# Delta rule: the first convolution tap moves to ScalarE, keys times beta becomes one VectorE operation, and the planner's durations follow

## The chip, the core and the metric

The kernel runs on one core of a Trainium2 chip. The core has TensorE (matrix products; the profile calls it PE, and PEld its loading of weights), VectorE (DVE), ScalarE (ACT), GpSimd (POOL) and SyncE (SP, which here only issues DMAs). Each engine takes its instructions strictly in the order of its own program and waits on semaphores for the others. The metric is the device time of one execution in microseconds; the median of several executions counts.

## What is computed

Two layers of one transformer block (convolutions, differential attention, SwiGLU) and then a second block with a gated delta rule, band attention, attention to a memory and SwiGLU, over 512 positions of width 1024, all in fp32. The change lies in the delta rule of the second block. Its part of the reference, cut to what matters:

```python
qkv = jax.nn.silu(_causal_dwconv(jnp.concatenate([qa, ka, va], axis=-1), conv_w[l]))   # 4 taps
q = _l2norm(...) * (A_DK ** -0.5);  k = _l2norm(...)          # 8 heads, chunks of 64
beta = sigmoid(beta);  g = -exp(a_log) * softplus(alpha + dt_bias);  G = cumsum(g)
L = where(strict, beta[..., :, None] * (k @ k.T) * decay, 0)
rhs = concatenate([beta[..., None] * v, (beta * exp(G))[..., None] * k], -1)
u_t, w = split(triangular_solve(I + L, rhs))
p_intra = (q @ k.T) * decay;  q_dec = q * exp(G);  k_dec = k * exp(g_last - G)
# scan over the 8 chunks: U = u_t - w @ S; o = q_dec @ S + p_intra @ U; S = S * e + k_dec.T @ U
```

The convolution has four taps per channel: position t gets tap 3 times itself plus taps 2, 1 and 0 times the three positions before it.

## The kernel before

Every large product is a *unit*: a weight matrix of 128 x 2048 numbers in `WR`, loaded by SP, split by ScalarE into a high part `WH` (step `split`, line 2191, one operation of 128 x 2048) and by GpSimd into a low part `WL` (step `low`, line 3036, eight operations of 128 x 256). TensorE multiplies activations (high and low part, `HH` and `HL`) with them at line 1894. The split of a unit waits until TensorE has finished the unit two before it, because the two share a buffer.

In the delta rule (`deltanet`) the projections of q, k and v come out of such units, and everything else is woven between them. For head h and j in q, k, v:

- `dq1` (VectorE, line 2783): the projection's bank times the row norm, into `pad`, of which there are two;
- `dq2` (VectorE), four steps with k = 3, 2, 1, 0: the first (line 2791) writes pad times tap 3 into `c`; it waits for `dq1` and, through `c_after`, for the readers of the old `c`. The others (line 2794) add one shifted tap each;
- `dq3` (ScalarE, line 2324): SiLU in place.

`prepare(h)` then makes what the solve and the scan need. In it `p9` multiplies the keys, which TensorE has turned into a bank, by the per-position factor in `RC[:, i, 2, h]`, one VectorE operation for each of four blocks of 128 columns, into `bk` (line 2840); ScalarE then makes `KD` from the same bank in four operations (line 2354). `invert(g)` solves for two heads at a time with 64 small products of 32 x 32 per step (lines 2034, 2044, 2053 and 2064), between which VectorE masks, subtracts and transposes (2868 to 2891). `scan(g)` runs the eight chunks (TensorE lines 2086, 2095, 2104 and 2112; VectorE 2906 and 2918; ScalarE 2377 and 2382).

The order of all steps is made at build time. `weave` keeps one clock per engine (`Clock`) and a lane for each generator, and always lets the lane go on whose last step ends first; the dense products are the first lane, whose time is that of TensorE. What a step costs on each engine is written in the table `ROUGH` (pairs of a fixed and a growing part, V for VectorE, A for ScalarE, T for TensorE). `Clock.run` starts a step when its engine is free and what it waits for is done. All engines' programs are emitted from the one list of steps, so a changed entry in `ROUGH` can change the order of instructions on each engine, but not their number.

Of the kernel before, what the change touches and what calls it, by code (L numbers as in the profile page):

```python
# [10 lines left out]
ALU = mybir.AluOpType  # L11
ACT = mybir.ActivationFunctionType
AX = mybir.AxisListType.X

P = 128
S = 512
# [78 lines left out]
def memory(nc, ctx):  # L95
# [153 lines left out]
    "gates1": ("V:ab", "A:beta"), "soft1": ("V:dtb", "A:edt", "A:alog"), "soft2": ("V:udt", "A:ldt"), "soft3": (),  # L249
    "gates3": ("V:dcum", "V:rg", "V:rlast", "A:reg", "A:rdec"),  # L250
    "gates4": ("A:rct",), "gates5": ("A:rhi", "V:rlo"),
    "nt": ("V:nt",), "dq1": ("V:dq1",), "dq2": ("V:dq2",), "dq3": ("A:dq3",),
    "p1": ("A:p1q",), "p2": ("A:pks",), "peq": ("V:peq",), "prow": (), "p4": ("V:p4a", "V:p4", "A:pdec"), "p4n": ("V:pkn",), "p4d": ("V:pdn",),
    "p5": (), "p6": ("V:psq",), "p6v": ("A:pbv",),
    "p8": (), "p9": ("V:pbk", "A:pkd"), "p11": (), "p12": ("V:pum",), "p13": (),
# [64 lines left out]
def by_dma(unit):  # L320
# [110 lines left out]
class Order:  # L431
# [6 lines left out]
    def step(self, kind, *key, **given):  # L438
        ends = self.pass_time(kind, key, given)
        for signal in KINDS[kind]:  # L440
            engine, name = signal.split(":")
            assert (name, key) not in self.value, (name, key)
            sem = SEMAPHORE.get(name, name)
            self.count[sem] = self.count.get(sem, 0) + 1
            self.value[name, key] = self.count[sem]
            self.last[engine] = (sem, self.count[sem])
            self.clock.when[self.last[engine]] = ends.get(engine, ends["end"])
        self.steps.append((kind, key, given))
# [42 lines left out]
    def at(self, name, *key):  # L491
        return SEMAPHORE.get(name, name), self.value[name, key]
# [49 lines left out]
def order(m):  # L542

    o = Order()
    at, step, now = o.at, o.step, o.now
# [6 lines left out]
    vec = lambda name, j=0: m.VECS[:, VEC[name] + j:VEC[name] + j + 1]  # L552
# [535 lines left out]
    def deltanet(fo, res_toks):  # L1088
# [57 lines left out]
        cfree = {n + str(i): f for n in "qkv" for i in range(2)}  # L1146
# [36 lines left out]
        def convolutions():  # L1183

            for h in range(8):
                for j in range(3):
                    while (h, j) not in pad_of:
                        yield
                    yield from until((read[j], h - 2))
                    pd = pad_of[h, j]  # L1190
                    for k in (3, 2, 1, 0):
                        step("dq2", h, j, k, pad=pd.i, tok=at("dq1", h, j), c_after=cfree["qkv"[j] + str(h % 2)])
                        if k == 0:
                            pd.free(at("dq2", h, j, 0))
                        yield
                    step("dq3", h, j)
                    curved[j].add(h)
                    yield
# [654 lines left out]
def blk(t, b):  # L1853
    return t[:, b * P:(b + 1) * P]


def v4(ap):
    return ap.rearrange("p (b q) -> p b q", q=P)
# [317 lines left out]
def scalar_program(nc, m, o, sems):  # L2176
    a, at = nc.scalar, o.at
    ae = Waits(a, sems)
    PB = m.PB
    vec = lambda name, j=0: m.VECS[:, VEC[name] + j:VEC[name] + j + 1]  # L2180
# [3 lines left out]
    for kind, key, w in o.steps:  # L2184
# [13 lines left out]
        elif kind == "gain":  # L2198
            site, c = key
# [11 lines left out]
        elif kind == "sq":  # L2211
            site, i, c = key
# [39 lines left out]
        elif kind == "glub":  # L2252
            l, j = key
            ae.wait_ge(*at("glu2", l, j))
            a.activation(m.ct[:], m.ct[:], ACT.Sigmoid, bias=vec(f"glu_b{l}", 2 + j)).then_inc(sems["glu3"], 1)
        elif kind == "lnact":
            l, j = key
            ae.wait_ge(*at("lnmul", l))
            a.activation(m.cc[j][:], m.cc[j][:], ACT.Silu, bias=vec(f"ln_b{l}", j), scale=vec(f"ln_g{l}", j)).then_inc(sems["lnact"], 1)
        elif kind == "qkin":  # L2260
            l, name, c = key
# [13 lines left out]
        elif kind == "sexp":  # L2275
            l, h, qb = key
            i, n = w["i"], P * (qb + 1)
            sums = (m.sm[:, 72 + 4 * h + qb:73 + 4 * h + qb], m.sm[:, 16 * i + 5:16 * i + 6])
            for j in range(2):
                ae.wait_ge(*at(f"smax{j}", *key))  # L2280
                ins = a.activation(m.pa[i][j][:, 0:n], m.pa[i][j][:, 0:n], ACT.Exp, bias=m.sm[:, 16 * i + j:16 * i + j + 1], scale=-1.0,
                                   accum_out=sums[j])
            ins.then_inc(sems["sexp"], 1)
        elif kind == "strans":
            l, h, qb = key
# [3 lines left out]
        elif kind == "spv":  # L2289
            l, h, qb = key  # L2290
# [26 lines left out]
        elif kind == "gates5":  # L2317
            ae.wait_ge(*at("rg"))
            a.activation(m.RHL[0:32, :], m.R[0:32, :], ACT.Copy)
            a.activation(m.RHL[64:96, :], m.R[64:96, :], ACT.Copy).then_inc(sems["rhi"], 1)  # L2320
        elif kind == "dq3":
            h, j = key
            ae.wait_ge(*at("dq2", h, j, 0))
            a.activation(m.cqkv[h % 2][j][:], m.cqkv[h % 2][j][:], ACT.Silu).then_inc(sems["dq3"], 1)
        elif kind == "p1":
            h, = key
# [3 lines left out]
        elif kind == "p2":  # L2330
            h, = key
            ae.wait_ge(*w["tile"].done)
            ae.all(w["after"])
            for i in range(4):
                ins = a.activation(blk(m.SQ[w["q"]], i), blk(PB[w["tile"].b], i), ACT.Square, accum_out=norms(h, 0)[:, i:i + 1])
# [4 lines left out]
        elif kind == "p6v":  # L2340
            h, = key
# [3 lines left out]
            for i in range(4):  # L2345
                ins = a.activation(blk(m.bv[h % 2], i), blk(PB[w["tile"].b], i), ACT.Copy, scale=norms(h, 2)[:, i:i + 1])
            ins.then_inc(sems["pbv"], 1)
        elif kind == "p9":
            h, = key
# [3 lines left out]
            for i in range(4):  # L2353
                ins = a.activation(m.KD[g][:, h % 2, i * P:(i + 1) * P], blk(PB[w["tile"].b], i), ACT.Copy, scale=norms(h, 3)[:, i:i + 1])
            ins.then_inc(sems["pkd"], 1)
        elif kind == "jd":
# [3 lines left out]
            for i in range(4):  # L2360
                rows = slice(32 * i, 32 * i + 32)
                ins = a.activation(diagonal(i, i), blocks(m.ZC[rows, :]), ACT.Copy)
# [4 lines left out]
        elif kind in ("i8u", "i8w"):  # L2367
            h, = key
# [15 lines left out]
        elif kind == "zact":  # L2384
            h, = key
            ae.wait_ge(*at("za1", h))
            a.activation(m.zs[h % 2][:], m.zs[h % 2][:], ACT.Silu).then_inc(sems["za"], 1)
        elif kind == "gact":
            c, = key
# [3 lines left out]
        elif kind == "bvin":  # L2393
            p, j = key
# [3 lines left out]
        elif kind == "bexp":  # L2398
            c, i, qb = key
# [4 lines left out]
        elif kind == "btrans":  # L2404
            c, i, qb = key
# [3 lines left out]
        elif kind == "bpv":  # L2409
            c, qb = key  # L2410
# [3 lines left out]
        elif kind == "gbact":  # L2414
            c, = key
            ae.wait_ge(*at("gb1", c))
            a.activation(m.SGB[:, c, :], m.SGB[:, c, :], ACT.Tanh, scale=0.5).then_inc(sems["gb"], 1)
        elif kind == "yop":
            _, c = key
# [7 lines left out]
        elif kind == "mssq":  # L2427
            c, = key
            ae.all(w["after"])
            a.activation(m.SQ[w["q"]][:, 0:256], m.MT[:, c, :], ACT.Square).then_inc(sems["mssq"], 1)  # L2430
        elif kind == "mop":
            _, c = key
# [3 lines left out]
        elif kind == "mvin":  # L2436
            u, j = key
# [4 lines left out]
        elif kind == "xexp":  # L2442
            h, qb = key
            i, j = h % 2, qb % 2
# [4 lines left out]
        elif kind == "xcopy":  # L2449
            h, = key  # L2450
# [4 lines left out]
        elif kind == "xpv":  # L2455
            h, k = key
# [5 lines left out]
def vector_program(nc, m, o, sems):  # L2462
    v, at = nc.vector, o.at
    ve = Waits(v, sems)
    dv = Chain(ve, "vchain")
    PB = m.PB
    ident = m.CON[:, C_ID:C_ID + P]
    vec = lambda name, j=0: m.VECS[:, VEC[name] + j:VEC[name] + j + 1]
# [33 lines left out]
    for kind, key, w in o.steps:  # L2502
# [3 lines left out]
        elif kind == "gain":  # L2506
            site, c = key
# [7 lines left out]
        elif kind == "sq":  # L2515
            site, i, c = key
# [7 lines left out]
        elif kind == "res":  # L2524
            name, c = key
# [52 lines left out]
        elif kind == "lam":  # L2578
# [3 lines left out]
            for j in range(2):  # L2582
# [3 lines left out]
                ins = v.tensor_reduce(sm[:, b + j:b + j + 1], sm[:, 64 + 64 * j:128 + 64 * j], AX, ALU.add)  # L2586
# [12 lines left out]
        elif kind == "glua":  # L2599
            l, j = key  # L2600
# [5 lines left out]
        elif kind == "glub":  # L2606
            l, j = key
            ve.all(w["after"])
            times_rstd(m.ct[:], w["tile"], "glu2")
        elif kind == "gluc":  # L2610
            l, j = key
# [7 lines left out]
        elif kind == "tap":  # L2619
            l, k, j = key  # L2620
# [163 lines left out]
        elif kind == "dq2":  # L2784
            h, j, k = key
            c, pad = m.cqkv[h % 2][j], m.pad[w["pad"]]
            tap = vec("conv2", 24 * k + 8 * j + h)
            if k == 3:
                ve.wait_ge(*at("dq1", h, j))
                ve.all(w["c_after"])  # L2790
                v.tensor_scalar(c[:], pad[:, 3:3 + S], tap, None, ALU.mult).then_inc(sems["dq2"], 1)
            else:
                ve.wait_ge(*at("dq2", h, j, k + 1))
                v.scalar_tensor_tensor(c[:], pad[:, k:k + S], tap, c[:], ALU.mult, ALU.add).then_inc(sems["dq2"], 1)
        elif kind == "p4":
            h, = key
            ve.wait_ge(*w["tile"].done)
# [37 lines left out]
        elif kind == "p9":  # L2835
            h, = key
            ve.wait_ge(*w["tile"].done)
            ve.all(w["after"])
            for i in range(4):
                ins = v.tensor_scalar(blk(m.bk[h % 2], i), blk(PB[w["tile"].b], i), m.RC[:, i, 2, h:h + 1], None, ALU.mult)  # L2840
            ins.then_inc(sems["pbk"], 1)
        elif kind == "p12":
            h, = key
            ve.wait_ge(*w["tile"].done)
# [385 lines left out]
```

## Time and profile before

| | us |
|---|---|
| median of 3 runs | 2467.93 (2467.66 to 2469.52) |
| the profiled execution | 2474.92 |
| its span in the trace | 2473.3 |

Busy shares of the span: PE 98%, PEld 81%, DVE 41%, ACT 38%, POOL 48%. Time is in us and duration of one operation in ns. The delta rule fills about 1160 to 1633 us of the span. A window row gives the busy time of each engine in that stretch with its count of instructions, then the granted TensorE clock (1.00 is 2.4 GHz; the other level is 1.2 GHz, so a mean between 0.5 and 1 is a mix), the DMA share and GB/s. In a timeline row, the bracket at the end is how long the engine was idle before the instruction and what released it.

### The profile page before, as it was taken

The page shows a single profiled execution, that of the slowest core. Times are in us where ns is not written, and L with a number is a line of the kernel's source. Part 1 is how long each engine was busy: PE and PEld are TensorE (multiplying, and loading weights), DVE is VectorE, ACT ScalarE, POOL GpSimd, SP SyncE. Part 2 cuts the span into 40 slices and gives each one's busy share as a digit, 9 for nine tenths or more (in the row PEclk, how much of TensorE's full clock was granted, in tenths as well). Part 3 has the DMA queues.
Part 4 walks back from the last instruction along what each step waited for, and adds up shares of the span by engine and source line. Part 5 has one row for each costly group of instructions (what it writes and reads, how often), then busy time and mean ns, then how long its engine had stood idle before and what let it go on. Part 6 is the DMA issues. An engine that isn't in the chain of part 4 may idle for free.

```text
span 2473.3 us, 35534 instructions
## 1 busy us (share of the span) xinstructions
PE 2428.1 (98%) x14295; PEld 2008.8 (81%) x14295; DVE 1005.1 (41%) x2261; ACT 935.2 (38%) x1435; POOL 1180.7 (48%) x1566
## 2 busy tenths in 40 slices
PE   8999999999999999999999999999999999999998
PEld 6888888888788888888888888877778888888887
DVE  7974111124874111123866775314435433211113
ACT  5553222224563322234543444225543434322221
POOL 5125655654115565655532233353326645655563
PEclk9999999999999999999999999999999999999999
DMA  5532223224642223224211111132213322223222
GB/s 178 138 103 86 102 88 109 100 76 131 162 103 86 103 81 115 85 88 142 94 54 53 53 52 53 69 136 77 86 60 120 115 91 91 97 86 110 102 80 83
DMA packets 42403, 237.17 MB, mean 96 GB/s; under 512 B 4736, under 2 KB 7936, under 8 KB 19712
## 3 DMA queue, kind: packets, MB, share of 16 engines
q1 hardware_dynamic: 39936, 218.13, 25.2%
q0 software_dynamic: 2304, 16.78, 3.3%
q8 instruction: 113, 1.85, 0.3%
q14 instruction: 50, 0.41, 0.1%
HBM read 213.92 MB, written 4.19 MB: 88 GB/s over the span
## 4 chain that ended last, share of the span: by engine, by line
PE 92%; DVE 3%; POOL 2%; issue 1%; DMA 1%; ACT 1%; SPq 0%; DVEq 0%; POOLq 0%; ACTq 0%
PE PB L1894 76%; PE PB L1896 4%; POOL WL L3036 1%; PE PB L1931 1%; PE PB L1906 1%; PE PB L2144 1%; PE PB L2125 1%; DVE cc L2622 1%; PE PB L1978 1%; PE PB L1995 1%; PE PB L2132 1%; DMA WR<-in_w_in 1%; PE PB L2156 1%; PE PB L2172 1%; PE PB L2086 0%
## 5 line engine op out<-in xcount | busy, mean ns | idle before, releaser
L3036 POOL TENSOR_TENSOR WL<-WR,WH 128x256 fp32r<-128x256 f32 (+1 forms) x1444 | 1053.1, 766 | 756.3 <-ACT WH L2191 756.3
L1894 PE MATMUL PB<-HH,WH 128*128 128x512 f32 x1992 | 797.4, 400 | 10.5 <-ACT HH L2206 10.0
L1894 PE MATMUL PB<-HL,WH 128*128 128x512 f32 x1992 | 781.0, 392 | 1.9 <-DVE HL L2514 1.9
L1894 PE MATMUL PB<-HH,WL 128*128 128x512 f32 x1992 | 517.4, 396 | 0.8 <-DMA WL<-WR 0.8
L2191 ACT ACTIVATE WH<-WR 128x2048 fp32r<-128x2048 f32 (+1 forms) x209 | 371.9, 1779 | 246.2 <-PE PB L1894 238.8
L1894 PEld LDWEIGHTS PB<-HH,WH 128*128 128x128 f32 x1992 | 376.9, 189 | 100.9 <-issue 13.7
L1894 PEld LDWEIGHTS PB<-HL,WH 128*128 128x128 f32 x1992 | 377.0, 189 | 78.1 <-DVE HL L2514 2.4
L1894 PEld LDWEIGHTS PB<-HH,WL 128*128 128x128 f32 x1992 | 366.8, 189 | 75.5 <-issue 2.0
L1894 PE MATMUL PB<-BL,WH 128*128 128x512 f32 (+1 forms) x859 | 331.3, 387 | 0.2 <-DVE BL L2523 0.2
L1894 PE MATMUL PB<-BH,WH 128*128 128x512 f32 (+1 forms) x795 | 308.1, 389 | 1.0 <-ACT BH L2226 1.0
L1894 PE MATMUL PB<-BH,WL 128*128 128x512 f32 (+1 forms) x795 | 195.1, 388 | 1.5 <-POOL WL L3036 1.5
L1894 PEld LDWEIGHTS PB<-BL,WH 128*128 128x128 f32 x859 | 161.4, 188 | 33.0 <-DVE BL L2523 0.5
L2529 DVE TENSOR_TENSOR X<-X,PB 128x512 f32<-128x512 f32 x79 | 54.2, 686 | 328.1 <-PE PB L1894 328.1
L1894 PEld LDWEIGHTS PB<-BH,WH 128*128 128x128 f32 x795 | 149.3, 188 | 31.6 <-ACT BH L2226 1.3
L1894 PEld LDWEIGHTS PB<-BH,WL 128*128 128x128 f32 x795 | 147.6, 188 | 33.2 <-POOL WL L3036 3.2
L3051 POOL TENSOR_TENSOR BL<-ff1c,BH 128x512 fp32r<-128x512 f32 x44 | 56.9, 1293 | 168.2 <-ACT BH L2226 168.2
L2226 ACT ACTIVATE BH<-ff1c 128x512 fp32r<-128x512 f32 x44 | 27.8, 632 | 233.4 <-DVE ff1c L2714 233.4
L2479 DVE TENSOR_TENSOR ff1b<-PB,RSTD 128x512 f32<-128x512 f32 x44 | 30.4, 691 | 196.5 <-PE PB L1894 196.5
L2479 DVE TENSOR_TENSOR ff1a<-PB,RSTD 128x512 f32<-128x512 f32 x44 | 30.4, 692 | 176.8 <-PE PB L1894 168.0
L3041 POOL DMA_DIRECT2D WL<-WR x16 | 14.1, 883 | 170.0 <-ACT WL L2194 170.0
L2622 DVE SCALAR_TENSOR_TENSOR cc<-cp,VECS,cc 128x512 f32<-128x512 f32 x120 | 92.0, 814 | 0.0
L2206 ACT ACTIVATE HH<-X,VECS 128x512 fp32r<-128x512 f32 x48 | 33.3, 717 | 106.2 <-DVE X L2529 106.2
(363 smaller groups left out, 2678.9 us busy)
## 6 DMA issues: line engine op xcount, KB each, us to landing
WR<-in_w_gu SPq DMA_DIRECT2D x66, 1024.0 KB, 4.7
WR<-in_w_dn SPq DMA_DIRECT2D x48, 704.0 KB, 4.0
WR<-in_w_in SPq DMA_DIRECT2D x22, 1024.0 KB, 4.7
WL<-WR POOLq DMA_DIRECT2D x16, 1024.0 KB, 7.0
WR<-in_qkv SPq DMA_DIRECT2D x12, 1024.0 KB, 4.7
WR<-in_w_out SPq DMA_DIRECT2D x8, 1024.0 KB, 4.7
WR<-in_qk SPq DMA_DIRECT2D x8, 1024.0 KB, 4.8
WR<-in_gb SPq DMA_DIRECT2D x4, 1024.0 KB, 4.7
```

The costliest lines, as they stand in the source:

```text
L1894: ins = pe.matmul(out[:, 0:n], wt[:, k * cols + j * P:k * cols + (j + 1) * P], x[:, k, t0:t0 + n], start=first, stop=last)
L1896: ins = pe.matmul(out[:, 0:cols], x[:, k, j * P:(j + 1) * P], wt[:, k * cols:(k + 1) * cols], start=first, stop=last)
L1906: ins = pe.matmul(out[:, j0 + b:j0 + b + 1], blk(src, b), ones[:, 0:1], start=(j0 == 0 and b == 0), stop=(b == nb - 1), skip_group_check=True)
L1931: ins = pe.matmul(blk(PB[t.b], i), blk(left, i), blk(right, i), start=True, stop=True)
L2191: a.activation(m.WH[u % 2][:, 0:n], m.WR[u % 2][:, 0:n], ACT.Copy).then_inc(sems["whi"], 1)
L2206: a.activation(m.HH[:, c, :], m.X[:, c, :], ACT.Copy, scale=w["gain"]).then_inc(sems["hh"], 1)
L2226: a.activation(high[:, w["c"], :], w["src"], ACT.Copy).then_inc(sems["bh"], 1)
L2479: v.tensor_tensor(dst, PB[t.b][:, 0:bank_cols], m.RSTD[:], ALU.mult).then_inc(sems[name], 1)
L2529: v.tensor_tensor(m.X[:, c, :], m.X[:, c, :], PB[w["tile"].b][:], ALU.add).then_inc(sems["res"], 1)
L2622: v.scalar_tensor_tensor(m.cc[j][:], m.cp[j][:, k:k + S], vec(f"dw_w{l}", 2 * k + j), m.cc[j][:], ALU.mult, ALU.add).then_inc(sems["tap"], 1)
L3036: g.tensor_tensor(m.WL[u % 2][:, part], m.WR[u % 2][:, part], f32(m.WH[u % 2][:, part]), ALU.subtract).then_inc(sems["wlo"], 1)
L3051: g.tensor_tensor(m.BL[:, w["c"], :], w["src"], f32(high[:, w["c"], :]), ALU.subtract).then_inc(sems["blg"], 1)
```

## The change

The first tap becomes a step of its own, `dq0`, a ScalarE Copy with a per-partition scale; the step `dq2` keeps the taps 2, 1 and 0. The wait for the readers of the old `c` goes with it to ScalarE. The four block operations of `p9` on VectorE become one with a broadcast operand. Five entries of `ROUGH` change.

```diff
-    "nt": ("V:nt",), "dq1": ("V:dq1",), "dq2": ("V:dq2",), "dq3": ("A:dq3",),
+    "nt": ("V:nt",), "dq1": ("V:dq1",), "dq0": ("A:dq0",), "dq2": ("V:dq2",), "dq3": ("A:dq3",),
...
-    "dq1": [("V", 0.72, 0)], "dq2": [("V", 0.78, 0)], "dq3": [("A", 1.105, 0)],
+    "dq1": [("V", 0.72, 0)], "dq0": [("A", 0.65, 0)], "dq2": [("V", 0.84, 0)], "dq3": [("A", 1.105, 0)],
...
-    "p9": [("V", 1.7, 0), ("A", 1.6, 0)],
+    "p9": [("V", 0.7, 0), ("A", 1.2, 0)],
...
-                    for k in (3, 2, 1, 0):
-                        step("dq2", h, j, k, pad=pd.i, tok=at("dq1", h, j), c_after=cfree["qkv"[j] + str(h % 2)])
+                    step("dq0", h, j, pad=pd.i, tok=at("dq1", h, j), c_after=cfree["qkv"[j] + str(h % 2)])
+                    yield
+                    for k in (2, 1, 0):
+                        step("dq2", h, j, k, pad=pd.i, tok=at("dq0", h, j))
...
+        elif kind == "dq0":
+            h, j = key
+            ae.wait_ge(*at("dq1", h, j))
+            ae.all(w["c_after"])
+            a.activation(m.cqkv[h % 2][j][:], m.pad[w["pad"]][:, 3:3 + S], ACT.Copy, scale=vec("conv2", 72 + 8 * j + h)).then_inc(sems["dq0"], 1)
...
-            if k == 3:
-                ve.wait_ge(*at("dq1", h, j))
-                ve.all(w["c_after"])
-                v.tensor_scalar(c[:], pad[:, 3:3 + S], tap, None, ALU.mult).then_inc(sems["dq2"], 1)
-            else:
-                ve.wait_ge(*at("dq2", h, j, k + 1))
-                v.scalar_tensor_tensor(c[:], pad[:, k:k + S], tap, c[:], ALU.mult, ALU.add).then_inc(sems["dq2"], 1)
+            ve.wait_ge(*(at("dq0", h, j) if k == 2 else at("dq2", h, j, k + 1)))
+            v.scalar_tensor_tensor(c[:], pad[:, k:k + S], tap, c[:], ALU.mult, ALU.add).then_inc(sems["dq2"], 1)
...
-            for i in range(4):
-                ins = v.tensor_scalar(blk(m.bk[h % 2], i), blk(PB[w["tile"].b], i), m.RC[:, i, 2, h:h + 1], None, ALU.mult)
-            ins.then_inc(sems["pbk"], 1)
+            v.tensor_tensor(v4(m.bk[h % 2][:]), v4(PB[w["tile"].b][:]), m.RC[:, :, 2, h:h + 1].broadcast_to([P, 4, P]), ALU.mult).then_inc(sems["pbk"], 1)
```

## Rows read from the trace of the kernel before

**Rows 1.** The page: busy shares of the engines, and the chain that ended last.
```profile
PE 2428.1 (98%) x14295; PEld 2008.8 (81%) x14295; DVE 1005.1 (41%) x2261; ACT 935.2 (38%) x1435; POOL 1180.7 (48%) x1566
...
PE 92%; DVE 3%; POOL 2%; issue 1%; DMA 1%; ACT 1%; SPq 0%; DVEq 0%; POOLq 0%; ACTq 0%
```

**Rows 2.** Windows: before the delta rule, and its middle in stretches of 60 us.
```profile
0.00:1150.00 1150.00, 1134.21 (x5356) 932.86 (x5357) 456.24 (x926) 431.56 (x579) 561.78 (x736) 1.00 0.34 107
...
1240.00:1300.00 60.00, 58.41 (x719) 48.39 (x720) 37.60 (x95) 25.54 (x51) 21.82 (x29) 0.94 0.16 54
1300.00:1360.00 60.00, 56.97 (x842) 48.07 (x841) 39.37 (x89) 23.04 (x51) 16.75 (x20) 0.91 0.16 54
1360.00:1420.00 60.00, 59.47 (x708) 51.27 (x706) 47.24 (x138) 25.98 (x53) 18.11 (x24) 1.00 0.16 54
1420.00:1480.00 60.00, 56.72 (x492) 49.65 (x492) 40.83 (x98) 28.28 (x59) 19.81 (x24) 0.91 0.16 54
1480.00:1540.00 60.00, 58.46 (x867) 49.47 (x866) 31.97 (x98) 25.27 (x45) 20.14 (x26) 0.97 0.14 48
```

**Rows 3.** Windows of 10 us around three falls of the granted clock.
```profile
1250.00:1260.00 10.00, 8.41 (x241) 5.97 (x242) 4.45 (x10) 2.15 (x2) 0.34 (x1) 0.66 0.02 5
...
1330.00:1340.00 10.00, 8.51 (x285) 7.28 (x284) 7.19 (x17) 4.66 (x8) 5.10 (x7) 0.86 0.02 5
1340.00:1350.00 10.00, 10.00 (x100) 7.93 (x99) 3.15 (x7) 2.00 (x5) 1.37 (x2) 0.63 0.31 107
...
1420.00:1430.00 10.00, 6.72 (x201) 5.63 (x201) 6.29 (x13) 3.94 (x6) 1.98 (x3) 0.62 0.01 3
1430.00:1440.00 10.00, 10.00 (x63) 9.11 (x61) 4.43 (x6) 3.76 (x12) 5.55 (x6) 0.86 0.32 107
```

**Rows 4.** Groups by line, 1160 to 1640 us: the operations that the change touches.
```profile
L2354 ACT ACTIVATE KD<-PB,SMALL 128x128 f32<-128x128 f32 x32 | 9.1, 367 | 28.3 <-DVE bk L2840 28.3
L2840 DVE TENSOR_SCALAR bk<-PB,RC 128x128 f32<-128x128 f32 x32 | 8.9, 339 | 0.0
L2791 DVE TENSOR_SCALAR cv<-pad,VECS 128x512 f32<-128x512 f32 x8 | 6.2, 779 | 0.1
L2791 DVE TENSOR_SCALAR cq<-pad,VECS 128x512 f32<-128x512 f32 x8 | 4.5, 562 | 0.1
L2791 DVE TENSOR_SCALAR ck<-pad,VECS 128x512 f32<-128x512 f32 x8 | 4.4, 546 | 0.0
```

**Rows 5.** Single lines, durations in ns (minimum/median/maximum): the nearest to what is added.
```profile
L2206 ACT ACTIVATE HH<-X,VECS x48: 702/723/727, 9.2 to 2101.0; 128x512 fp32r<-128x512 f32 x48
...
L2329 ACT ACTIVATE SQ<-cq x8: 612/616/635, 1202.1 to 1488.6; 128x512 f32<-128x512 f32 x8
...
L2801 DVE TENSOR_TENSOR PB<-PB,RC x8: 689/690/693, 1197.2 to 1474.5; 128x512 f32<-128x512 f32 x8
```

**Rows 6.** Waits of ScalarE, 1160 to 1640 us: total us, times, longest.
```profile
ACT WH L2191 <- PE PB L1894: 60.8, 14, 16.6
...
ACT KD L2354 <- DVE bk L2840: 28.3, 7, 6.3
```

**Rows 7.** Timeline: four instructions on one chain, and three other gaps of PE.
```profile
1408.51 1.13 DVE L2840 TENSOR_SCALAR bk<-PB,RC 128x128 f32<-128x128 f32 x4
...
1409.67 1.14 ACT L2354 ACTIVATE KD<-PB,SMALL 128x128 f32<-128x128 f32 x4 [5.51 <-DVE bk L2840]
1410.84 0.41 ACT L2377 ACTIVATE UT<-UU 64x256 f32<-64x256 f32 x1
...
1411.30 0.71 PE L2112 MATMUL PB<-PT,UT 128*128 128x128 f32 x4 [0.53 <-ACT UT L2377]
...
1252.24 0.32 PE L2034 MATMUL PB<-TC,UM 32*32 32x32 f32 x4 [1.59 <-issue]
...
1316.17 0.74 PE L2034 MATMUL PB<-TC,UM 32*32 32x32 f32 x64 [1.54 <-DVE TC L2873]
...
1337.29 0.54 PE L2044 MATMUL PB<-ZC,YC 32*32 32x32 f32 x22 [1.10 <-issue]
```

4 rows, old and new, of the table ROUGH are left out of this document.

## The prediction

> **What bounds the kernel now.** I read the page first. TensorE is busy 98% of the span and holds 92% of the chain that ended last, and VectorE and ScalarE are busy only 41% and 38% [rows 1]. So an operation taken from VectorE or given to ScalarE is worth nothing by itself; it is worth what TensorE loses by waiting for it. Next come the windows, to see where TensorE loses anything at all. All that the change touches lies in the delta rule, about 1160 to 1633 us. Before it, in 1150 us, the granted clock is full [rows 2]. In the middle of the delta rule, five stretches of 60 us, two losses can be read [rows 2]. First, idle time: 60 minus the PE busy time of each gives 1.6 + 3.0 + 0.5 + 3.3 + 1.5 = 9.9 us. Second, clock: 60 times (1 minus granted clock) gives 3.6 + 5.4 + 0 + 5.4 + 1.8 = 16.2 us that went by at the lower level and were not worked off. Together these 26 us are all that any reordering of this stage can win; the same two can also grow.
>
> The clock is lost in a few falls, not evenly. One costs 10 x 0.34 = 3.4 us (1250 to 1260), one 10 x (0.14 + 0.37) = 5.1 us (1330 to 1350), one 10 x (0.38 + 0.14) = 5.2 us (1420 to 1440) [rows 3]. Each began in a window with 201 to 285 PE instructions (many small products, little dense work) in which TensorE was also idle for 1.5 to 3.3 us. Whether one gap tips the clock can't be said from the trace: the gap of 1.54 us at 1316 [rows 7] lies some 15 us ahead of the nearest fall [rows 3]. A fall is worth 3 to 5 us, as much as this kernel's measurement can tell from nothing, which I take as 0.2%, or 4.9 us. So the outcome hangs more on whether a fall vanishes or is added than on the work moved.
>
> **The first tap.** Taken from VectorE: 24 operations, 6.2 + 4.5 + 4.4 = 15.1 us [rows 4]. The mean is 0.63 us. Given to ScalarE: 24 Copies of 128 x 512 with a scale read from `VECS`. The trace has that form at line 2206 (same shape, same kind of scale, another output type): 0.723 us; without such a scale ScalarE takes 0.616 us (line 2329) [rows 5]. I take 0.72, the nearer form, so 24 x 0.72 = 17.3 us are added to ScalarE, or 14.8 us at the lower price. In the five stretches ScalarE is busy 25.5 + 23.0 + 26.0 + 28.3 + 25.3 = 128 of 300 us and VectorE 37.6 + 39.4 + 47.2 + 40.8 + 32.0 = 197 of 300 [rows 2]. The busier engine is relieved and the idler one loaded, which is cover for most of it. If the cover were gone the edit would cost 17.3 - 15.1 = 2.2 us.
>
> **The new wait.** Tap 2 on VectorE now waits for ScalarE, where before it waited only for VectorE itself. Behind tap 2 in VectorE's queue stand the masks, subtractions and transposes of the inversion, the scan's updates and the next `dq1`, and TensorE waits for each of those. What can hold ScalarE up ahead of `dq0` is above all the split of the next weight: ScalarE stood 14 times at line 2191 for TensorE, 60.8 us together and up to 16.6 us once [rows 6]. The order puts a split right after the unit that it waits for, so when the split is released, TensorE has only just begun the next unit; the delay that VectorE then sees is the split itself and `dq0`. The planner knows both and places tap 2 after `dq0` by its clock (0.65 against the 0.72 that I expect, a lapse of 0.07 us each). The hand-over itself is short: `KD` started 0.03 us after `bk` ended (1408.51 + 1.13 to 1409.67) [rows 7]. So the wait costs between nothing, where other steps come first, and, where the planner's clock is ahead of the real one, 1 to 2 us of VectorE each time. Most of those don't reach TensorE, which has dense products in between. I take +1 us in all, with 0 and +8 as ends.
>
> **Keys times beta.** Four operations of 0.339 us, overlapping, took 1.13 us from end to end [rows 4, 7], and 8.9 us in all eight heads. One operation with a broadcast operand from the same `RC` on a bank takes 0.690 us at line 2801 [rows 5]. 8 x 0.69 = 5.5, so VectorE is relieved of 3.4 us, and `KD`, which waited 28.3 us in 7 heads for `bk` [rows 6], starts 0.44 us sooner where the rest is in time. Once this can be followed to TensorE: `bk`, `KD`, the scan's copy `UT` and the product at 1411.30, which stood idle for 0.53 us [rows 7]. There 0.44 us, and the first tap just ahead of `bk` on VectorE, make the gap go away: -0.5 us. The chain behind the gap at 1316 (1.54 us) is VectorE's masking after `DT`, with no first tap or `p9` in it, and the gaps at 1252 and 1337 (1.59 and 1.10 us) came in the middle of a burst of small products, ended by the issue of instructions and by no other engine [rows 7]. I leave these three where they are. For the other idle time (9.9 less 0.5 and 4.2, so 5.2 us), which is partly ended by VectorE, a relief of VectorE by (15.1 + 3.4)/197 = 9% may take up to a third: between 0 and -1.7 us; I take -1.
>
> **The estimates.** VectorE's share of `p9` falls from 1.7 to 0.7 (it was 1.13, it will be about 0.69) and ScalarE's from 1.6 to 1.2 (1.14 in the trace [rows 7]). The planner thus loses a cushion of some 1 us per head behind which a late VectorE could hide, and gets a truer clock. The order changes from the first head on, on every engine. Nothing in the trace prices that; it can't be more than the 26 us pool on the good side, and on the bad side the nearest rows are the falls of the clock, one added being 3.4 to 5.2 us. For the likeliest case I take -2 us: half a fall of the smallest kind, because VectorE has less queued in just those stretches. This is the weakest term.
>
> **Sum.** +1.0 - 0.5 - 1.0 - 2.0 = -2.5 us on the profiled execution's 2474.92, thus 2472.4. That execution lies 7.0 us above the median of the three runs; the change doesn't touch that difference, so the median goes from 2467.93 to 2465.4.
>
> **A rule that speaks against the change.** VectorE did the first tap in 0.63 us on average, and ScalarE will need about 0.72 for it [rows 4, 5]: if engine time counted for itself, the edit would lose 2.2 us (rival 4). The Trainium skill ("ScalarE: Activation LUTs", section "Rules for kernel authors") says that multiplications are VectorE's work and not ScalarE's. By that rule, the trace agrees on the price of one operation; that the busier engine gives it away is what the rule leaves out, and the sum above goes by that.
>
> **The rivals.**
> 1. *The small gain* above, 2465.4, own range 2463 to 2472: the order changes, the falls stay about as they are. For it: TensorE is covered nearly everywhere. It includes that the change does nothing that can be measured, 2467.9.
> 2. *A fall of the clock vanishes.* VectorE, 79% busy in 1360 to 1420 [rows 2], gets ahead, and one or two of the three falls in rows 3 go, with some 2 us of the idle time next to them: -3.4 - 2 = -5.4 to -5.2 - 5.1 - 2 = -12.3, thus 2455.6 to 2462.5, and 2459 as its middle. For it: each fall stands beside idle time. Against it: 2.7 us of that idle time is `issue`, which the change doesn't reach.
> 3. *The wait behind the split.* `dq0` stands behind a split (line 2191) or behind ScalarE's other waits, tap 2 holds VectorE's queue, and TensorE comes to a product of the inversion or scan before its operand. With a fourth of the 24 taps hit and 0.7 us of it seen by TensorE each, 4.2 us, and one fall added for it, 3.4 us: +7.6, thus 2475.5. It decides from the point where VectorE is less than about 2 us ahead of TensorE; the gaps of 0.53 and 1.54 us [rows 7] show that there is no lead at all in places. Against it: ScalarE is busy only 43% of the stage and the planner counts the split.
> 4. *The multiplication belongs on VectorE.* The extra 2.2 us of engine time reach TensorE and the relief doesn't: 2470.1. Against it: no gap in rows 7 is ended by ScalarE's amount of work.
>
> **How the numbers follow.** Chances: small gain or nothing 0.42, a fall vanishes 0.32, the wait behind the split 0.20, the rule 0.06. Predicted is the first, 2465.4. The range has to reach into cases 2 and 3 until a tenth is left at either end: 2456 to 2476. Faster by over 0.2% means below 2463.0: case 2, and a little of case 1: 0.33. Slower by over 0.2% means above 2472.9: case 3 and the tail of the others: 0.21. The rest, 0.46, is within 0.2%.
>
> **What would show it.** In the new profile: 24 ScalarE Copies from `pad` at 0.72 us and `bk` in eight operations of about 0.69 us; 72 VectorE taps left. VectorE's idle time ended by `dq0` (tap 2 waiting for ScalarE) is the new wait: under 5 us in all bears out case 1 or 2, over 10 us, with gaps of TensorE ended by VectorE right behind, case 3. The windows of 60 us tell the rest: idle time below 8 us and clock loss between 12 and 20 us is case 1; a clock loss below 12 us is case 2. The prediction is wrong in its mechanism if the time changes outside 1160 to 1640 us, and wrong in its weakest term if the clock loss moves by more than 5 us either way.

## The result and the profile after

| | before | after |
|---|---|---|
| median of 5 runs, us | 2467.66 (2464.60 to 2469.52) | 2483.98 (2483.43 to 2487.14) |
| ratio, 95% interval | | 1.0067 (1.0056 to 1.0077) |
| profiled execution, us | 2474.92 | 2483.43 |
| its span, us | 2473.3 | 2482.1 |

The change made the kernel 16.3 us slower by the medians; forecast were 2465.4 us and a range of 2456 to 2476. The two profiled spans differ by 8.8 us only, because the profiled execution of the kernel before was 7 us above its median. The page of the changed kernel, busy shares and chain of the end, to be held against [rows 1]:

```profile
PE 2428.1 (98%) x14295; PEld 2005.6 (81%) x14295; DVE 988.9 (40%) x2213; ACT 949.7 (38%) x1459; POOL 1175.0 (47%) x1566
...
PE 88%; DVE 5%; POOL 2%; issue 2%; ACT 2%; DMA 1%; SPq 0%; DVEq 0%; POOLq 0%; ACTq 0%
```

VectorE is busy 16.2 us less and ScalarE 14.5 us more, and TensorE is busy for the same 2428.1 us. But VectorE's share of the chain that ended last rose from 3% to 5% and ScalarE's from 1% to 2%: an engine was relieved, and yet a larger part of the chain stands on it. Windows of the changed kernel, as in [rows 2] (busy us of PE, PEld, DVE, ACT and POOL, then the granted clock, DMA share and GB/s):

```profile
0.00:1150.00 1150.00, 1134.23 (x5352) 932.94 (x5353) 454.62 (x925) 430.58 (x577) 561.93 (x736) 1.00 0.33 107
...
1240.00:1300.00 60.00, 57.59 (x775) 47.23 (x775) 34.07 (x87) 29.27 (x54) 17.67 (x25) 0.94 0.15 54
1300.00:1360.00 60.00, 55.93 (x849) 47.27 (x848) 36.64 (x85) 26.23 (x58) 18.64 (x24) 0.94 0.14 47
1360.00:1420.00 60.00, 54.33 (x623) 46.52 (x625) 43.57 (x123) 28.19 (x56) 18.07 (x24) 0.98 0.18 61
1420.00:1480.00 60.00, 58.94 (x565) 50.41 (x566) 34.50 (x86) 27.43 (x56) 16.43 (x23) 0.93 0.10 36
1480.00:1540.00 60.00, 55.21 (x824) 45.94 (x823) 29.45 (x83) 24.60 (x49) 14.93 (x20) 0.91 0.16 54
```

Up to 1150 us nothing has changed. From 1240 to 1540 us TensorE is idle for 2.4 + 4.1 + 5.7 + 1.1 + 4.8 = 18.0 us instead of 9.9 [rows 2]. The clock loss is 3.6 + 3.6 + 1.2 + 4.2 + 5.4 = 18.0 us instead of 16.2. The waits of TensorE, 1160 to 1650 us (total us, times, longest):

```profile
PE PB L2046 <- DVE YC L2877: 6.5, 2, 4.2
PE PB L2066 <- issue: 2.9, 2, 1.9
PE PB L1916 <- DVE zc L2500: 2.7, 1, 2.7
```

The kernel before had no such wait above 2.2 us in total in that stretch. The one of 4.19 us, in the timeline of TensorE and VectorE:

```profile
1412.12 1.20 PE L1896 MATMUL PB<-HH,WL 128*128 128x512 f32 x4
...
1413.92 0.73 PE L1896 MATMUL PB<-HH,WL 128*128 128x512 f32 x2
1414.99 0.75 PE L2036 MATMUL PB<-TC,UM 32*32 32x32 f32 x64 [0.34 <-DVE TC L2882]
1419.93 1.07 PE L2046 MATMUL PB<-ZC,YC 32*32 32x32 f32 x64 [4.19 <-DVE YC L2877]
```

```profile
1407.89 0.69 DVE L2486 TENSOR_TENSOR pad<-PB,RSTD 128x512 f32<-128x512 f32 x1
...
1414.87 0.65 DVE L2852 TENSOR_TENSOR PT<-PB,DT 128x512 f32<-128x512 f32 x1
1415.44 0.67 DVE L2859 TENSOR_TENSOR QD<-cq,PB 128x512 f32<-128x512 f32 x1
...
1419.37 0.42 DVE L2877 TENSOR_TENSOR YC<-PB,CON 128x256 f32<-128x256 f32 x1
...
1422.92 0.74 DVE L2796 SCALAR_TENSOR_TENSOR cq<-pad,VECS,cq 128x512 f32<-128x512 f32 x1
1423.70 0.69 DVE L2486 TENSOR_TENSOR pad<-PB,RSTD 128x512 f32<-128x512 f32 x1
```

Two things are to be seen. First, TensorE's last dense products before the wait are over at 1414.65, and none is queued between the product at 1414.99 and its successor at 1419.93. VectorE never stands still meanwhile: it works through the steps `p14` (line 2852), `p15` (2859, 2860), `p6` (2829 to 2832) and a tap and then comes to the mask `YC`. In the kernel before it did the same steps at 1412.3 to 1416.2, with the mask `YC` ahead of the tap, while TensorE had dense products to do:

```profile
1412.27 0.68 DVE L2852 TENSOR_TENSOR PT<-PB,DT 128x512 f32<-128x512 f32 x1
...
1416.14 0.41 DVE L2877 TENSOR_TENSOR YC<-PB,CON 128x256 f32<-128x256 f32 x1
1416.48 0.74 DVE L2794 SCALAR_TENSOR_TENSOR cq<-pad,VECS,cq 128x512 f32<-128x512 f32 x1
1417.25 0.69 DVE L2479 TENSOR_TENSOR pad<-PB,RSTD 128x512 f32<-128x512 f32 x1
```

```profile
1412.71 0.50 PE L1894 MATMUL PB<-HH,WH 128*128 128x512 f32 x1
...
1416.48 1.52 PE L1894 MATMUL PB<-HH,WL 128*128 128x512 f32 x6
1417.93 0.75 PE L2044 MATMUL PB<-ZC,YC 32*32 32x32 f32 x64
```

Second, from one filling of a pad to the next, 1407.89 to 1423.70, 15.8 us pass, and the second comes directly after the last tap that gives a pad back (1422.92 + 0.74). That alone proves nothing: in the kernel before the same interval was 14.2 us (from 1403.01) and ended in the same way. So the question for the experiments was: what took the dense products away from there?

### The profile page after: what moved, and what is told of

Its sections match the earlier page's. It is cut to its first block, busy times and chain, and to the rows that moved or that the text cites. A ratio compares the mean times of both kernels' runs of the same rounds, so it can differ in the third digit from the quotient of the medians.

```text
span 2482.1 us, 35517 instructions
## 1 busy us (share of the span) xinstructions
PE 2428.1 (98%) x14295; PEld 2005.6 (81%) x14295; DVE 988.9 (40%) x2213; ACT 949.7 (38%) x1459; POOL 1175.0 (47%) x1566
## 3 DMA queue, kind: packets, MB, share of 16 engines
HBM read 213.92 MB, written 4.19 MB: 88 GB/s over the span
## 4 chain that ended last, share of the span: by engine, by line
PE 88%; DVE 5%; POOL 2%; issue 2%; ACT 2%; DMA 1%; SPq 0%; DVEq 0%; POOLq 0%; ACTq 0%
PE PB L1896 73%; PE PB L1898 4%; POOL WL L3036 2%; PE PB L1933 1%; PE PB L1908 1%; PE PB L2146 1%; PE PB L2127 1%; DVE cc L2629 1%; PE PB L1980 1%; PE PB L1997 1%; PE PB L2134 1%; DMA WR<-in_w_in 1%; PE PB L2158 1%; PE PB L2174 1%; ACT WH L2193 1%
```

## The experiments

**Operations against order.** A changed entry of `ROUGH` changes the order of the list. With care in the entries, the list of steps of the kernel before can be kept, word for word, under the changed operations, and the other way round. Theory O: the order costs the 16 us. Rival W, from the prediction: VectorE's queue waits for ScalarE at tap 2.

*x_ops*, the changed operations in the order of before:

```diff
-    "dq0": [("A", 0.65, 0)], "dq2": [("V", 0.84, 0)]
+    "dq0": [("V", 0.78, 0)], "dq2": [("V", 0.78, 0)]
...
-    "p9": [("V", 0.7, 0), ("A", 1.2, 0)]
+    "p9": [("V", 1.7, 0), ("A", 1.6, 0)]
```

> The changed kernel's operations in the order of the kernel before: first tap on ScalarE, keys times beta as one VectorE operation, but the planner keeps its old entries (the tap planned as 0.78 us of VectorE, p9 as before), so the list of steps is the same as before. Theory O (the order is what costs): the 16 us do not appear; within 4 us of the kernel before (2467.7), rather 1 to 3 us faster. Rival W (VectorE's queue waits for ScalarE at tap 2): at least half of the 16 us appears, 2476 or more, and VectorE shows over 10 us of idle time ended by the ScalarE tap.

Measured: 2473.20 us against 2468.78, ratio 1.0013 (1.0002 to 1.0025). That is 4.4 us above the kernel before measured beside it, or 0.4 us outside theory O's 4 us, and not the gain of 1 to 3 us; it is below rival W's 2476. Rival W's other sign did appear (below).

*x_order*, the operations of before in the order of the changed kernel: `dq0` is planned as ScalarE's and done by VectorE.

```diff
-    "dq0": ("A:dq0",)
+    "dq0": ("V:dq0",)
...
+        elif kind == "dq0":       # in vector_program
+            v.tensor_scalar(m.cqkv[h % 2][j][:], m.pad[w["pad"]][:, 3:3 + S], vec("conv2", 72 + 8 * j + h), None, ALU.mult)
...
-            v.tensor_tensor(v4(m.bk[h % 2][:]), ...)
+            for i in range(4):
+                ins = v.tensor_scalar(blk(m.bk[h % 2], i), blk(PB[w["tile"].b], i), m.RC[:, i, 2, h:h + 1], None, ALU.mult)
+            ins.then_inc(sems["pbk"], 1)
```

> The mirror image: all operations as before (first tap on VectorE, four block operations for the keys), in the order of the changed kernel. Theory O: the loss is all here, 2480 to 2488, with the same large gaps of TensorE. Rival W: no ScalarE tap, so no wait for it; 2466 to 2472.

Measured: 2486.38 us, ratio 1.0065 (1.0052 to 1.0079). The windows of this kernel, and two of its waits of TensorE:

```profile
1360.00:1420.00 60.00, 54.32 (x679) 46.66 (x677) 46.10 (x132) 24.79 (x51) 19.23 (x24) 0.97 0.16 54
1420.00:1480.00 60.00, 58.94 (x510) 50.43 (x511) 36.36 (x94) 26.24 (x57) 18.98 (x24) 0.95 0.10 36
1480.00:1540.00 60.00, 55.22 (x820) 45.87 (x819) 30.78 (x93) 24.20 (x41) 13.74 (x19) 0.91 0.16 54
```

```profile
PE PB L2046 <- DVE YC L2879: 6.5, 2, 4.2
PE PB L1916 <- DVE zc L2495: 2.7, 1, 2.7
```

TensorE's busy time is the same as in the changed kernel to 0.01 us in each of the three windows, and the waits of 4.2 and 2.7 us are there, without one changed operation. The order carries the loss; theory O holds for the loss, and rival W falls as its cause. The wait of W exists all the same: with the order held still, VectorE stood for ScalarE's tap 5 times, 15.9 us together (rows of x_ops, waits of VectorE), against 1.9 us in the changed kernel, whose planner knew of the tap.

```profile
DVE cv L2796 <- ACT cv L2327: 10.1, 2, 7.5
DVE cq L2796 <- ACT cq L2327: 5.8, 3, 3.2
```

**The two parts.** *x_tap* is the first part alone with its own entries (`dq0`, `dq2`), *x_key* the second alone with its own (`p9`); the other part is as before in each.

> Only the first part of the change, planned anew: the tap on ScalarE with its entries of the table (0.65 on ScalarE, 0.84 for the other taps); keys and p9 as before. Theory O: each new table gives another order, and the time follows the order, not the work moved; the planner lets the dense products stand at a held pad more often here than in the changed kernel, so slower than the changed kernel too, 2485 to 2500. Rival W: no slower than the changed kernel, since the wait is the same: 2480 to 2485.

Measured: 2499.84 us, ratio 1.0120 (1.0104 to 1.0136). The tap's part alone is 15.9 us slower than the whole change, so the new entry of `p9` isn't neutral beside it: with the tap's entries it moved the order to a better one.

> Only the second part of the change, planned anew: keys times beta as one VectorE operation with p9 planned as 0.7 and 1.2; the first tap stays on VectorE. Theory O: the order changes a little, and with it the time, 2464 to 2474. Rival W: nothing waits for ScalarE, 3.4 us of VectorE are relieved, 2464 to 2468.

Measured: 2468.16 us, ratio 0.9997 (0.9988 to 1.0006). That is within theory O's range and just above W's, so it doesn't part the two. Without the tap there is no loss, and by x_order it is the tap's planning and not its operation.

In the order of before, the parts were also measured by themselves. *x_ops_tap* is x_ops with the keys in four operations; *x_ops_key* is the kernel before with this one edit:

```diff
-            for i in range(4):
-                ins = v.tensor_scalar(blk(m.bk[h % 2], i), blk(PB[w["tile"].b], i), m.RC[:, i, 2, h:h + 1], None, ALU.mult)
-            ins.then_inc(sems["pbk"], 1)
+            v.tensor_tensor(v4(m.bk[h % 2][:]), v4(PB[w["tile"].b][:]), m.RC[:, :, 2, h:h + 1].broadcast_to([P, 4, P]), ALU.mult).then_inc(sems["pbk"], 1)
```

> In the order of the kernel before, the first tap alone on ScalarE (keys times beta in four operations). Measures the new wait against VectorE's relief with the order held still. Mine: the wait eats the relief, 2468 to 2474. Rival: the version with both operations lost its 3 us by something else, 2464 to 2467.

> In the order of the kernel before, keys times beta alone as one VectorE operation; first tap on VectorE. Mine: nothing can get later, 3.4 us of VectorE are relieved and the gap of 0.5 us at 1411 goes: 2465 to 2468. Rival: bk is written all at once and later products see it no sooner, or a fall of the clock moves: 2469 to 2473.

Measured: 2466.76 us, ratio 0.9997 (0.9987 to 1.0007), and 2469.87 us, ratio 1.0006 (0.9994 to 1.0018). Neither can be told from no change, so both expectations, mine of a loss for the tap and of a gain for the keys, came out as nothing (both medians lie in the ranges of their rivals). That both together, x_ops, show 0.13% follows from neither. The granted clock of the executions accounts for most of it: span times (1 minus granted clock) is 16.8 us on average in the 9 executions of x_ops and 13.1 us in the 19 of the kernel before taken beside them, and the spans without it are 2454.8 and 2454.1 us.

**Why that order.** `convolutions()` is one lane of `weave`: for each of the 24 pairs of head and q, k, v it goes through the first tap, three taps and SiLU, and starts the next pair only then. The lane goes on when its last step ends by the planner's clock, and a step ends when its engine's queue has come to it. Before, a round passed ScalarE's queue once (SiLU); after, twice. The last tap gives the pad back; while both pads are held, `project` yields without a step, and no dense product is put into the list. The other lanes go on, and their small products then stand in TensorE's program without dense ones between them. Theory L is that this serial lane makes the loss. Rival R: every order other than the present one is worse, by chance. Rival P: two pads are too few.

*x_own*: the changed kernel, in which the tap has a lane of its own.

```diff
+        def first_taps():
+            for h in range(8):
+                for j in range(3):
+                    while (h, j) not in pad_of:
+                        yield
+                    yield from until((read[j], h - 2))
+                    step("dq0", h, j, pad=pad_of[h, j].i, tok=at("dq1", h, j), c_after=cfree["qkv"[j] + str(h % 2)])
+                    first.add((h, j))
+                    yield
...
         def convolutions():
-                    while (h, j) not in pad_of:
+                    while (h, j) not in first:
                         yield
-                    yield from until((read[j], h - 2))
-                    step("dq0", h, j, ...)
```

> The changed kernel, same operations and same table, but the ScalarE tap is issued by a lane of its own as soon as its pad is full, not inside the serial convolution lane. Theory L (the convolution lane is serial, and the tap makes each of its 24 rounds pass ScalarE's queue twice; the pads are held longer, the dense products stand at a held pad and TensorE reaches the small products too early): most of the 16 us comes back, 2465 to 2474, and TensorE's idle time from 1180 to 1540 us falls from 18.8 to 9 to 13 us. Rival R (any other order than the carefully tuned one is slower by 10 to 30 us): stays at 2480 or above.

Measured: 2465.04 us, ratio 0.9991 (0.9982 to 1.0000). All of the loss is gone, with the same operations and the same entries. Rival R falls with it.

*x_planv*: the changed kernel with one entry other.

```diff
-    "dq0": [("A", 0.65, 0)]
+    "dq0": [("V", 0.78, 0)]
```

> The changed kernel with one entry of the table other: the ScalarE tap is planned as 0.78 us of VectorE, as the tap was before; the new entries for the other taps and for p9 stay. The operations are those of the changed kernel. Theory L: planning the tap in ScalarE's queue is what lengthens the rounds, so 10 or more of the 16 us come back, 2469 to 2475. Rival R: 2480 or above. If the new entries of the other taps and of p9 were the cause, it would stay at 2480 too.

Measured: 2468.35 us, ratio 0.9999 (0.9989 to 1.0010), a little better than expected. So the entry of the new step makes the loss, and not that of `p9`, to which I gave the weight in the prediction. VectorE stood 21.7 us for ScalarE's tap here (12.8 us for `cq`, 8.9 us for `cv`), and the time is that of the kernel before: once more against W.

*x_pads*: the changed kernel with a third pad.

```diff
-    m.pad = (pad0, pad1)
+    pad2, = run(216704, 222688, ("pad2", [P, 3 + S]))
+    m.pad = (pad0, pad1, pad2)
...
-        pads = Ring([Room(0), Room(1)], clock)
+        pads = Ring([Room(0), Room(1), Room(2)], clock)
```

> The changed kernel with a third pad. Rival P (two pads are too few, the dense products only lack a buffer): 2466 to 2474. Theory L: a third pad makes the projections run further ahead, but the serial lane behind them is as slow as before, so the wait comes later and nothing is won: 2480 to 2495.

Measured: 2503.58 us, ratio 1.0140 (1.0126 to 1.0154). Rival P falls: a third pad doesn't help. It is 9 us slower than even theory L expected. My reading is that with a third pad the projections run ahead, and more of the serial lane is left over with no dense product beside it. Its windows agree (no idle time of TensorE from 1240 to 1300 us, then 7.3 + 8.1 + 6.8 + 8.4 us in the next four of 60 us), but no experiment tests it.

*x_slow*: the kernel before, no operation changed; SiLU after the taps is only planned longer.

```diff
-    "dq3": [("A", 1.105, 0)]
+    "dq3": [("A", 2.5, 0)]
```

> The kernel before, not one operation changed; only SiLU after the taps is planned as 2.5 us of ScalarE instead of 1.105 (it takes 0.63). That makes each of the 24 rounds of the serial convolution lane 1.4 us longer in the planner's clock, about what the ScalarE tap did. Theory L: the same loss without the change: 2476 to 2490, TensorE idle for 15 us or more from 1180 to 1540. Rival R (chance of the order, or the tap itself): 2464 to 2472.

Measured: 2481.40 us against 2466.52, ratio 1.0053 (1.0038 to 1.0068). The loss appears without the change, by making the rounds longer on paper. (SiLU takes 0.63 us in fact.) On paper everything that waits for SiLU is later here too, `prepare` among it; it is x_own and x_silu (next), which change the lanes alone, that single out the lane.

*x_silu* and *x_key3*: SiLU gets the lane of its own, in the changed kernel and in the version with the keys alone.

```diff
                         if k == 0:
                             pd.free(at("dq2", h, j, 0))
+                            summed.add((h, j))
                         yield
-                    step("dq3", h, j)
-                    curved[j].add(h)
-                    yield
+        def silus():
+            for h in range(8):
+                for j in range(3):
+                    while (h, j) not in summed:
+                        yield
+                    step("dq3", h, j, tok=at("dq2", h, j, 0))
+                    curved[j].add(h)
+                    yield
```

> The changed kernel, same operations, with SiLU taken out of the serial convolution lane into one of its own; the ScalarE tap stays in it. Theory L: one ScalarE step per round again, so as in the kernel before or a little better, 2461 to 2470. Rival R: 2480 or above.

Measured: 2457.73 us against 2466.52, ratio 0.9957 (0.9945 to 0.9970). It has all operations of the change, beats both kernels and lies 3.3 us below the expected range. Its windows:

```profile
1240.00:1300.00 60.00, 58.78 (x741) 49.72 (x728) 38.77 (x96) 33.24 (x66) 23.52 (x28) 1.00 0.15 54
1300.00:1360.00 60.00, 59.01 (x873) 49.89 (x872) 41.29 (x93) 29.93 (x58) 21.64 (x27) 1.00 0.16 54
1360.00:1420.00 60.00, 59.69 (x873) 49.94 (x871) 41.53 (x119) 25.79 (x52) 19.42 (x27) 1.00 0.18 62
1420.00:1480.00 60.00, 59.18 (x628) 51.34 (x630) 42.17 (x113) 33.69 (x70) 17.69 (x24) 1.00 0.17 59
1480.00:1540.00 60.00, 59.84 (x634) 51.22 (x621) 28.26 (x84) 23.23 (x41) 20.68 (x27) 1.00 0.12 42
```

Idle are 1.2 + 1.0 + 0.3 + 0.8 + 0.2 = 3.5 us, and the clock doesn't fall in these windows (over the whole execution it was 0.997). So 3.5 of the 26 us that the prediction had counted here are left, by order and not by moved work. The gain is smaller than that difference: 16.9 us between the two profiled spans and 8.8 us between the medians, since the kernel before loses less clock in most of its executions than in its profiled one (see the base of the sum, below).

> A version meant to beat both: the first tap stays on VectorE, keys times beta is one VectorE operation with its new entry, and SiLU after the last tap gets a lane of its own, so that a round of the convolution lane holds four VectorE steps and no ScalarE step. Theory L: the rounds get shorter than in the kernel before, TensorE's idle time from 1180 to 1540 us falls below the 8.2 us of the version with the keys alone, 2455 to 2464. Rival R: 2470 or above.

Measured: 2464.79 us, ratio 0.9982 (0.9973 to 0.9991). Faster than before, but just outside the expected range; its lane is the fastest of all (table) and the time isn't, so there something else is last; no run here shows what.

**How they stand together.** The last tap's start is from the line of the taps, `cv`, in each trace; idle and clock loss are sums over the six windows of 60 us from 1180 to 1540, made as in the prediction. The last two columns are no times of the chip; they are read out when the list of steps is built. "At held pads" is how long, by the planner's clock, the lane of dense products stood in `project` because every pad was held. The planner's end is TensorE's time in `Clock` after the last step. The list of steps of x_ops, x_ops_tap and x_ops_key is that of the kernel before in all 5848 steps (with `dq0` read as the first tap), and that of x_order is the changed kernel's.

| | ratio to before | last tap starts, us | PE idle, us | clock loss, us | at held pads | planner's end |
|---|---|---|---|---|---|---|
| x_silu | 0.9957 | 1450.2 | 3.8 | 0 | 9.2 | 2508.1 |
| x_key3 | 0.9982 | 1446.8 | 7.1 | 3.6 | 0.9 | 2503.7 |
| x_own | 0.9991 | 1469.3 | 6.4 | 5.4 | 23.3 | 2515.8 |
| x_key | 0.9997 | 1474.7 | 8.2 | 6.6 | 43.8 | 2515.3 |
| x_ops_tap | 0.9997 | 1475.8 | 8.1 | 4.8 | 45.4 | 2513.7 |
| x_planv | 0.9999 | 1481.6 | 9.9 | 10.8 | 35.7 | 2519.8 |
| before | 1 | 1483.8 | 10.0 | 16.2 | 45.4 | 2513.7 |
| x_ops_key | 1.0006 | 1478.5 | 10.6 | 5.4 | 45.4 | 2513.7 |
| x_ops | 1.0013 | 1486.2 | 11.7 | 13.8 | 45.4 | 2513.7 |
| x_slow | 1.0053 | 1486.8 | 17.8 | 13.8 | 66.2 | 2532.5 |
| x_order | 1.0065 | 1493.5 | 18.8 | 15.6 | 61.6 | 2536.7 |
| after | 1.0067 | 1494.9 | 18.8 | 18.0 | 61.6 | 2536.7 |
| x_tap | 1.0120 | 1513.7 | 30.7 | 21.0 | 72.6 | 2552.4 |
| x_pads | 1.0140 | 1511.9 | 31.4 | 24.6 | 39.5 | 2544.3 |

With two pads, the column of held pads goes with the loss: all four kernels above 60 us lose 0.5% or more, and none of the nine up to 46 us does. x_pads, with three pads, doesn't fit that column. The last tap's start differs by 10 us among the four kernels with one list of steps, so a few us of that column mean nothing.

Two of the rows from which the third column comes, before and after (one line of the kernel; durations in ns, first and last start):

```profile
L2794 DVE SCALAR_TENSOR_TENSOR cv<-pad,VECS,cv x24: 735/752/1141, 1195.0 to 1483.8; 128x512 f32<-128x512 f32 x24
```

```profile
L2796 DVE SCALAR_TENSOR_TENSOR cv<-pad,VECS,cv x24: 708/752/1290, 1196.4 to 1494.9; 128x512 f32<-128x512 f32 x24
```

## Why the prediction was wrong, point by point

- **What bounds the kernel**: right. TensorE's busy time is the same in both profiled executions, and its idle time grew by 8.9 us in all (2473.3 - 2428.1 to 2482.1 - 2428.1), 8.8 of them in the six windows of the delta rule. That moved work is worth nothing by itself held too: x_ops has 15 us less on VectorE than the kernel before, and no gain.
- **The first tap**: the price was right; the changed kernel's rows say 0.712 to 0.726 us. The totals moved less than the forecast: ScalarE's busy time grew by 14.5 us (17.3 forecast), and VectorE's fell by 16.2 us (18.5 forecast, with the keys).

```profile
L2327 ACT ACTIVATE cv<-pad,VECS 128x512 f32<-128x512 f32 x8 | 5.8, 726 | 0.1
L2327 ACT ACTIVATE cq<-pad,VECS 128x512 f32<-128x512 f32 x8 | 5.7, 717 | 0.0
L2327 ACT ACTIVATE ck<-pad,VECS 128x512 f32<-128x512 f32 x8 | 5.7, 712 | 0.0
L2841 DVE TENSOR_TENSOR bk<-PB,RC 128x512 f32<-128x512 f32 x8 | 5.4, 677 | 0.0
```

- **The new wait**: right in size for VectorE's queue (+1 us with ends of 0 and +8). VectorE stood for the tap for 1.9 us in three places in the changed kernel. By the sign that I wrote down, under 5 us, that spoke for case 1 or 2, and the time was worse than case 3; and where VectorE did stand for it, 15.9 us (x_ops) and 21.7 us (x_planv), the time hardly moved or didn't. So the sign was of no use. I counted the wait only in VectorE's queue. The same wait stood a second time in the planner's lane, where it delays 24 rounds one behind the other; that was missed.
- **Keys times beta**: the price was right, 0.677 us against 0.69, and 5.4 us for 8.9. `KD`'s wait for `bk` fell from 28.3 to 11.5 us. The 0.5 us of TensorE that I followed from it can't be told apart: in x_ops_key the same product waits 0.15 us instead of 0.53 us (line 2112, at 1406), and in the old order neither part alone, nor both, gave a gain in time.
- **The estimates**: this is the step that failed. It was called the weakest term and yet had a sign and a price, -2 us, and a bad side bounded by one fall of the clock, 3.4 to 5.2 us. Measured is +16.0 us by the ratio and +17.6 us by the medians for the order alone (x_order). The sign was taken from "VectorE has less queued", which isn't how this planner decides; the bound was taken from single falls of the clock, while TensorE's idle time grew as well, from 10.0 to 18.8 us in the six windows. And I put the trouble down to the entry of `p9`; it was the entry of the new step that did it (x_planv), by making each of 24 serial rounds longer in the planner's clock.
- **The rivals**: none named the cause. The third came nearest, with less than half of the loss (+7.6 us of 16.3), by another mechanism, which x_order excludes. The wait that the edit adds to every round of a lane stood in the diff, one `yield` further than I read it.
- **The rule that speaks against the change**, that multiplications are VectorE's (the Trainium skill, "ScalarE: Activation LUTs", section "Rules for kernel authors"), didn't decide either: with the order kept, the tap on ScalarE cost nothing that could be measured (x_ops_tap), and x_silu, which has it there, is the fastest kernel of the study.
- **The base of the sum**: the 16.2 us of clock loss were those of one execution, 7 us above the median, and one of the worst: the 67 executions of the kernel before that were taken beside the experiments had granted clocks of 0.991 to 0.997, and the profiled one had 0.991. Span times (1 minus granted clock) is 12.9 us on average in the 67, and 21.9 us in the five of the changed kernel; the spans without it are 2453.7 and 2461.7 us. So of the 17 us between the mean spans about 9 are clock and about 8 are the rest, which agrees with the 8.8 us of idle time. (The clock is recorded to 0.001, which is 2.5 us of one execution.) The bad side of the weakest term, one fall of 3.4 to 5.2 us, was too small for the first and had nothing for the second.

## What to carry to other kernels

Where a program orders the instructions from a table of durations, a changed step has three costs: its duration, its wait, and its place in the planner's lanes; hold the order still and change the operations, then the other way round, and the last is separated from the first two in two experiments. A serial generator whose rounds each enter an engine's queue is a chain like any other: count how often a round enters a busy queue, and give a step that nobody in the round needs a lane of its own. Here the planner's own end was later by 18.8 us or more for every kernel that lost 0.5% or more and by 6.1 us at most for all others (table), so it is worth reading before an entry is believed to be harmless.

## What the runs showed of the hardware

- From 1180 to 1540 us the granted clock fell in very different measure at nearly the same idle time: 16.2, 13.8, 5.4 and 4.8 us were lost in the profiled executions of four kernels with the same list of steps and 8.1 to 11.7 us of idle time, and nothing at 3.8 us of idle time (x_silu). All kernels with more than 17 us of idle time lost 13.8 us or more.
- The spread of one kernel's time goes with the granted clock: of the 67 executions of the kernel before, the seven at 0.997 took 2461.2 to 2466.8 us and the six at 0.991 or 0.992 took 2472.0 to 2474.8 us.
- A ScalarE Copy with a scale read from a tile took 0.72 us where the Square of the same size without one took 0.616 [rows 5], in 24 of 24 cases within 0.02 us of the price taken from another line.
